# Second stage of a decoder layer in the order of use, with its first weights loaded in the stage before

## What is computed

```python
z = rmsnorm(x) @ w_in                        # q, kc, vc, ks, vs, kw, vw, gates, ...
def compress(t, pos, w1, w2):                # t is kc or vc: 2 groups of 64 columns
    blocks = t[:, win] + pos                 # 127 blocks of 32 tokens, one every 16
    return gelu(blocks.reshape(..., 32 * 64) @ w1) @ w2
kcmp, vcmp = compress(kc, ...), compress(vc, ...)
o_cmp = softmax(q @ kcmp - slope * dist) @ vcmp         # these scores also choose 8 blocks of 64 keys
o_sel = attention of q over the chosen blocks of ks, vs
o_win = attention of q over the last 512 keys of kw, vw
y_nsa = g0 * o_cmp + g1 * o_sel + g2 * o_win            # g = sigmoid(gates + gate_b)
```

## Time and profile before

| | us |
|---|---|
| median of 3 runs | 4426.35 |
| the profiled execution's own time | 4413.77 |
| its span | 4412.0 |
| first stage | 0 to 1562.0 |
| second stage | 1562.0 to 1645.4 |
| third stage until PE's first matmul | 1645.4 to 1663.3 |

### The profile page before, as it was taken

How to read it: one execution, slowest core, us unless ns; L and a number is a source line. 1 busy time by engine, 2 the same in 40 slices (tenths; PEclk the granted TensorE clock), 3 DMA queues, 4 the chain that set the end, 5 groups by cost and what they waited for, 6 DMA issues and landing times. The chain is left out here.

```text
span 4412.0 us, 69857 instructions
## 1 busy us (share of the span) xinstructions
PE 3913.7 (89%) x26848; PEld 3202.0 (73%) x26849; DVE 2436.8 (55%) x4140; ACT 1986.3 (45%) x3138; POOL 550.6 (12%) x842
## 2 busy tenths in 40 slices
PE   7899999999988848988888876999589999999698
PEld 5687877777766626777776765899578888888487
DVE  2454555555465426777766644444567555567465
ACT  2433333443332315666665643222166555566465
POOL 0111121111122002111111111000110000001110
PEclk9999999999999958999999966999789999999799
DMA  4443443433423250000000004433288666689542
GB/s 134 130 114 100 135 116 93 129 104 86 120 75 87 54 119 22 13 13 17 13 20 18 20 10 138 134 129 120 86 336 302 235 235 235 234 306 380 203 147 90
DMA packets 512951, 557.22 MB, mean 126 GB/s; under 512 B 106284, under 2 KB 374572, under 8 KB 511628
## 3 DMA queue, kind: packets, MB, share of 16 engines
q1 hardware_dynamic: 471476, 457.94, 32.6%
q0 software_dynamic: 16416, 59.78, 3.6%
q10 hardware_dynamic: 24784, 35.71, 2.5%
HBM read 439.78 MB, written 113.57 MB: 125 GB/s over the span
## 5 line engine op out<-in xcount | busy, mean ns | idle before, releaser
L523 PE MATMUL fr_fb<-fr_hT_h,fr_w_h 128*128 128x512 f32 (+1 forms) x1312 | 530.3, 404 | 7.7 <-DVE fr_hT_r L978 6.0
L523 PE MATMUL fr_fb<-fr_hT_r,fr_w_h 128*128 128x512 f32 (+1 forms) x1312 | 529.0, 403 | 0.0
L523 PE MATMUL fr_fb<-fr_hT_h,fr_w_r 128*128 128x512 f32 (+1 forms) x1312 | 528.2, 403 | 0.0
L958 DVE TENSOR_TENSOR fr_w_r<-fr_w_raw,fr_w_h 128x1024 fp32r<-128x1024 f32 (+1 forms) x164 | 197.7, 1206 | 487.6 <-ACT fr_w_h L774 486.5
L1911 DVE TENSOR_TENSOR aq_p_lo<-aq_t_bank,aq_p_hi 128x512 fp32r<-128x512 f32 x412 | 282.8, 689 | 225.9 <-ACT aq_p_hi L1804 220.0
L1804 ACT CAST aq_p_hi<-aq_t_bank 128x512 fp32r<-128x512 f32 x412 | 238.0, 581 | 293.7 <-PE aq_t_bank L1709 290.7
L798 ACT COPY fr_zs<-fr_fb 128x512 f32<-128x512 f32 (+1 forms) x148 | 87.1, 589 | 503.0 <-PE fr_fb L523 502.6
L523 PEld LDWEIGHTS fr_fb<-fr_hT_h,fr_w_h 128*128 128x128 f32 (+1 forms) x1312 | 246.8, 188 | 71.6 <-issue 10.4
L523 PEld LDWEIGHTS fr_fb<-fr_hT_h,fr_w_r 128*128 128x128 f32 (+1 forms) x1312 | 246.8, 188 | 62.8 <-issue 11.0
L134 PE MATMUL ex_gu<-wx_gate_w,ex_xT 128*128 128x512 f32 x1176 | 289.1, 402 | 3.0 <-DVE ex_xT L2667 3.0
L523 PEld LDWEIGHTS fr_fb<-fr_hT_r,fr_w_h 128*128 128x128 f32 (+1 forms) x1312 | 247.2, 188 | 61.3 <-issue 9.6
(11 more groups left out here) (474 smaller groups left out, 8787.5 us busy)
## 6 DMA issues: line engine op xcount, KB each, us to landing
wx_raw<-in_w_exp_gate_up SPq DMA_DIRECT2D x64, 2048.0 KB, 10.4
fr_w_raw<-in_w_in SPq DMA_DIRECT2D x160, 512.0 KB, 3.9
wx_raw<-in_w_exp_down SPq DMA_DIRECT2D x32, 2048.0 KB, 11.1
s_z<-fr_zs SPq DMA_DIRECT2D x160, 256.0 KB
s_rows<-ex_y ACTq DMA_DIRECT2D x50, 512.0 KB, 4.4
mx_mg<-s_z SPq DMA_DIRECT2D x32, 512.0 KB, 7.3
fr_zc<-s_z SPq DMA_DIRECT2D x15, 903.0 KB, 6.7
fr_x_t<-in_x SPq DMA_DIRECT2D x16, 512.0 KB, 5.5
```

Of the source, the lines that this page charges most:

```text
L523: ins = pe.matmul(bank[0:cols_, :], (w_h, w_h, w_r)[p][:, k, c, 0:cols_].bitcast(F32R), (hT_h, hT_r, hT_h)[p][:, c, :].bitcast(F32R), star ...
L958: dve.tensor_tensor(w_r[:, m % 2, :, 0:cols_].bitcast(F32R), w_raw[:, m % 2, :, 0:cols_], w_h[:, m % 2, :, 0:cols_], ALU.subtract).then_in ...
```

## The change

1. **A shared buffer.** `fr_x_t` becomes `sh_shared`, which lives through the first three stages. In its first 2080 columns `w1` and `pos` are placed, and in the third stage `t_sel`, `qf`, `t_cmp`, `keep_t` and `force_t` lie in it (`t_sel` over `w1` and `pos`, so it is still built in the third stage).
2. **Early weights.** SP issues the eight DMAs of `w1` and `pos` in the first stage, at the start of block 13, no longer ACT in the second.
3. **Order of use in the second stage.** `kv` of K is SP's first load and `kv` of V is ACT's first. PE multiplies with `pos` first, then `kv` of K, `kv` of V, V groups 0 to 3, the products with `w2`, V groups 4 to 7, the gates. ACT follows: gelu, 8 copies of V, then the four parts of K.
4. **Queries and tables.** The q loads of t = 15 and 14, the first three `qf`, both q splits and all tables but `t_sel` move into the second stage. `tab_ok` and the three waits for it go.

```diff
+                if c == NCH - 3:
+                    sync.wait_ge(filled, last_turn[NQ - 1] + 1)
+                    for a, n in enumerate(("k", "v")):
+                        for d in range(2):
+                            own = slice(d * HD, (d + 1) * HD)
+                            sync.dma_start(early["w1"][own, a, :, :], A[f"cmp_{n}_w1"][0]...).then_inc(early["in_w1"], 16)
+                            sync.dma_start(early["pos"][own, a, :], A[f"cmp_pos_{n}"][0]...).then_inc(early["in_w1"], 16)
...
             @block.sync
             def _(sync):
...
+                load_kv(sync, 0)
                 for br in range(2):
-                    sync.dma_start(v_raw[:, br, :], ...).then_inc(in_v, 16)
+                    sync.dma_start(v_raw[:, br, :], ...).then_inc(in_v[br], 16)
+                load_raw(sync, 0)
+                load_qf(sync, 0)
                 load_k(0)
                 load_k(1)
                 sync.dma_start(g_raw[:, :], Z["gate"]).then_inc(in_g, 16)
                 sync.dma_start(gate_b[:, :], ...).then_inc(in_g, 16)
+                load_raw(sync, 1)
                 load_k(2)
                 load_k(3)
+                for o in range(1, QF):
+                    load_qf(sync, o)
...
             @block.scalar
             def _(act):
...
+                load_kv(act, 1)
                 act.dma_start(w2_v[:, :], A["cmp_v_w2"][0]).then_inc(in_w, 16)
...
-                pe.wait_ge(tab_ok, 1)
...
-                act.wait_ge(tab_ok, 1)
...
-                dve.wait_ge(tab_ok, 1)
```

More of the change, by code:

```diff
@@ L1650, in _, with turn_v @@
                     masked(pair[:, :], [[-1, HD]], -d * HD, 1, 1.0, ALU.not_equal)
-                pool.sem_inc(tab_ok, 1)
+                split_q(pool, 0)
+                split_q(pool, 1)
+            @block.tensor
+            def _(pe):
+                def turn_v(n):
+                    pe.wait_ge(in_v[n // 4], 16)
+                    if n >= 4:
+                        pe.wait_ge(v_ok, n - 3)
+                    for t in range(4):
+                        ins = pe.transpose(tp[:, n % 4, t * P:(t + 1) * P],
+                                           v_raw[:, n // 4, (n % 4 * 4 + t) * P:(n % 4 * 4 + t + 1) * P], ident[:, :])
+                    ins.then_inc(turned, 1)
+                pe.wait_ge(in_w1, 16 * 8)
+                for a in range(2):
+                    for l in range(HALF):
+                        ins = pe.matmul(out[0:HD, POS + a:POS + a + 1], w1[:, a, l, :], pos[:, a, l:l + 1],
+                                        start=(l == 0), stop=(l == HALF - 1))
+                    ins.then_inc(pos_made, 1)
+                for a in range(2):
+                    both = acc[0:HD, a, 0:G * P].rearrange("p (g j) -> p g j", g=G)[:, :, 0:N_CMP]
+                    pe.wait_ge(in_kv[a], 32)
+                    for l in range(HALF):
+                        ins = pe.matmul(both, w1[:, a, l, :], kv[:, a, :, l:l + CMP_STRIDE * (N_CMP - 1) + 1:CMP_STRIDE],
+                                        start=(l == 0), stop=(l == HALF - 1))
+                    ins.then_inc(hid_made, 1)
+                pe.wait_ge(id_ok, 2)
+                for n in range(4):
+                    turn_v(n)
+                pe.wait_ge(hid_ok, 2 * G)
+                pe.wait_ge(in_w, 16 * 3)
+                for g in range(G):
+                    pe.matmul(out[:, 0:N_CMP], w2_k[:, g, :], hid[:, 0, g, :], start=(g == 0), stop=(g == G - 1))
+                for g in range(G):
+                    ins = pe.matmul(out[0:N_CMP, (2 + g) * P:(2 + g) * P + HD], hid[:, 1, g, :], w2_v[:, :],
+                                    start=True, stop=True)
+                ins.then_inc(out_made, 1)
+                for n in range(4, 8):
+                    turn_v(n)
+                pe.wait_ge(in_g, 32)
+                for t in range(NT):
+                    ins = pe.transpose(gp[:, t * N_GATE:(t + 1) * N_GATE], g_raw[:, t * P:(t + 1) * P],
+                                       ident[0:N_GATE, 0:N_GATE])
+                ins.then_inc(g_made, 1)
@@ new lines, in _, with high @@
+            @block.scalar
+            def _(act):
+                def high(i):
+                    br, g = i // G, i % G
+                    act.wait_ge(in_k[i % 2], 32 * (i // 2 + 1))
+                    act.copy(k_hi[:, br, g, :].bitcast(F32R), k_raw[:, i % 2, :]).then_inc(k_high, 1)
+                load_kv(act, 1)
+                act.dma_start(w2_v[:, :], A["cmp_v_w2"][0]).then_inc(in_w, 16)
+                act.wait_ge(w2_clear, 1)
+                for g in range(G):
+                    act.dma_start(w2_k[:, g, g * HD:(g + 1) * HD], A["cmp_k_w2"][0]).then_inc(in_w, 16)
+                act.wait_ge(pos_made, 2)
+                for a in range(2):
+                    act.copy(pos_p[:, a:a + 1], out[0:HD, POS + a:POS + a + 1]).then_inc(pos_ok, 1)
+                for a in range(2):
+                    act.wait_ge(hid_made, a + 1)
+                    act.wait_ge(pos_ok, a + 1)
+                    for g in range(G):
+                        act.activation(hid[:, a, g, :], acc[0:HD, a, g * P:g * P + N_CMP], ACT.Gelu_apprx_tanh,
+                                       bias=pos_p[:, a:a + 1]).then_inc(hid_ok, 1)
+                for n in range(8):
+                    act.wait_ge(turned, n + 1)
+                    act.copy(v2[:, n // 4, n % 4 * 4:n % 4 * 4 + 4, :, 0:HD].bitcast(F32R),
+                             tp[:, n % 4, :].rearrange("p (t g d) -> p t g d", t=4, g=G)).then_inc(v_high, 1)
+                high(0)
+                high(1)
+                act.wait_ge(g_ok, 1)
+                act.activation(gates[:, :, :], gates[:, :, :], ACT.Sigmoid).then_inc(g_done, 1)
+                high(2)
+                high(3)
+                act.wait_ge(g_done, 1)
@@ L3021, in build_program @@
         Z["passed"], Z["whole"] = passed, whole
-        stage_front(nc, A, Z)
-        stage_nsa(nc, A, Z)
+        with ExitStack() as both:
+            sh = Stage(nc, both, "sh")
+            shared = sh.sb("shared", [P, QCH, D])
+            early = dict(w1=shared[:, 0:2, :].rearrange("p a (l e) -> p a l e", e=HD),
+                         pos=shared[:, 2, 0:2 * L_HALF].rearrange("p (a l) -> p a l", a=2),
+                         in_w1=sh.lasting_sem("in_w1", whole))
+            stage_front(nc, A, Z, shared, early)
+            stage_nsa(nc, A, Z, shared, early)
         stage_moe(nc, A, Z)
```

357 lines of the change are left out of this document (149 added, 208 removed).

## The result

The changed kernel takes 4394.3 us (median of 4 runs, 4391.0 to 4401.6), the kernel before 4425.8 (4 runs, 4422.8 to 4428.9): a ratio of 0.9929 with a 95% interval of 0.9916 to 0.9942, or 31.5 us less (26 to 37). I forecast 4404.0 within 4392 to 4418, and gave faster by over 0.2% a chance of 0.87. The time fell in the range; the gain was 31.5 us where I had 22.4.

What follows compares the result with a forecast made beforehand. The prediction saw the second stage waiting for loads, then PE idle behind POOL's q split and tables. First attention matmul at 1640.9 instead of 1663.3 gains 22.4 us, less 0 in the first stage: 4426.35 - 22.4 = 4404.0, range 4392 to 4418.

Steps and rivals of the forecast that it cites:

- What bounds the kernel: Second stage waits for loads until about 1609; then PE idles 19.33 us behind POOL's q split and tables.
- The tables: Tables and q splits run on idle POOL under second-stage loads; PE no longer waits for them entering the third stage.
- The sum: First attention matmul at 1640.9 instead of 1663.32, a gain of 22.4 us, less 0 in the first stage.
- T: Start of the second stage, its first `kv` DMA; 1562.0 in the forecast's time line.
- The kv loads: Second stage's front: queues share 208 GB/s evenly, so K's and V's pairs land together at 1584.
- rival 1: Second stage: K's `kv` pair lands first, at 1574; gain 32.4 us, time 4394; chance 0.17.
- V: Second stage, behind the gelu: ACT's last V copy at 1619.5, within 1618.1 to 1621.8.
- K: Second stage's end: third and fourth K loads wait for `k_raw`'s buffers; last low part at 1640.0 instead of 1644.6.
- The change of stage: From DVE's last copy in the second stage to the third stage's first matmul: 0.9 us, giving 1640.9.
- `pos`: Second stage: PE's 4.6 us of products with `pos` run while `kv` is awaited, so hidden.
- The first stage: Block 13: the eight weight DMAs hold SP until about 1351, 4 us before the inverses' trip; 0 lost.
- rival 3: Block 13: small pieces starve the recurrence; slower by 0.2% needs 5.5 ns per piece, 60 us held gives 4450; chance 0.03.

Runs made afterwards that it cites:

- e1: Changed kernel with q's loads, both splits and the tables back in the third stage; 4409.1 us, ratio 0.9970 to before.
- e11: Kernel of e4 with K's `kv` pair first on both queues (lower half SP, upper ACT) and V's pair behind; 4381.4 us, ratio 0.9913.
- e4: Changed kernel with the first two K parts split between the two gelus; 4379.5 us, ratio 0.9908 to before.
- e2: Changed kernel with the eight `w1` and `pos` DMAs back on ACT's queue in the second stage, ahead of V's pair; 4426.5 us, ratio 1.0006.
- e5: Changed kernel with a second set of the eight weight DMAs behind the first in block 13; 4398.9 us, ratio 0.9944 to before.

## Why the prediction was right, and what was mis-sized

**What bounds the kernel: right.** Both stretches that I named were on the path. Undoing one costs 17.2 us, undoing the other 30.7.

**The tables: right.** I gave the moved tables and q the whole 17.9 us of idle time behind the stage; e1 gives 17.2. The cover that I named for q and the splits was there with room.

**The sum, step by step.** From T to attention I forecast 78.9 us and it took 72.65. The 6.3 us come from the first two terms; the others were met:
- *The kv loads*, 3.9 us. I took 1584 for both pairs, or +22, by an even share. The rate was right (220 where I had 208), the share was not: SP's pair ended 5.4 us ahead of ACT's. The first product started at +18.1, between the forecast and rival 1's +12, since V's pair is not needed until the second product. Rival 1's mechanism was at work in part. I had treated it as a case of its own and the even share as the likely one, with no row on either. That the median of 4394.3 is rival 1's 4394 is chance: its condition, K's pair at +12, did not come true, and even with K first on both queues (e11) it is there only at +15.2. One reading was wrong: the trace of before does have two queues with 64-partition loads in flight. From 1603.83, when SP issues K loads, to 1608.1, when V's upper half lands on ACT's queue, 204 GB/s move. So the 208 of the earlier trace rows is not `kv` alone, and it agrees with the rule on the halves; how two queues share is still not in it.
- *V*, 2.3 us. From the first product to ACT's last V copy I had 35.5 us and it took 33.2. The transposes took 1.97 us for 16, where the earlier trace rows has 3.65 at 1.2 GHz; PE had come from 27.6 us of work, and from 1621.2 to 1626.2 its granted clock is 1.00 (2.4 GHz). I knew the lower end of that range (1618.1) and took a value 1.4 us above it. The other 0.9 us lie below that end: mostly the products with `w2`, which held PE for 1.0 us (1623.16 to 1624.18) where I had 2.2.
- *K*: 20.5 us forecast from the last V copy to the last low part, 20.4 measured. The reload behind `k_raw`'s two buffers was the end of the stage, as the prediction had it, and e4 shows that it was so by order alone: it gives 12.3 us back by splitting two parts while ACT and DVE stood idle. The prediction said that nothing hides these loads, and did not ask what else could.
- *The change of stage*: 0.9 and 0.9.
- *`pos`* was hidden, as forecast, but it takes 6.96 us at 1.2 GHz and not 4.6; e2 shows it when it is not hidden.

**The first stage: nearly right.** I took nothing lost. SP was held 10.3 us instead of 7.6 to 8.2, mostly by one of `pos` (3.13 us). The margin of the trip was all but used up (SP is free at 1366.73 and issues the trip at 1367.41); but the trip itself took 2.8 us more, its pieces being in the queue with the weights' last ones, and that step I had not looked at. It cost DVE 1.2 us and PE 1.35. e5 shows that the price of one more microsecond there is about one, as rival 3 says; its 5.5 ns a piece was far from the 1.3 measured (10.3 us for 8192).

**The rest.** 28.7 us in the second stage less 1.2 in the first are 27.5; the medians differ by 31.5, with an interval of 26 to 37. The 4 us between are within that interval and within the scatter of the rest: in thirteen profiled executions the way from the first attention matmul to the end takes 2747.2 to 2758.6 us, and in the changed kernel's it is 2.9 us longer than in before's, not shorter. Where the 4 us come from stays open.

## What to carry to other kernels

When a stage is shortened at its front, list what was hidden under that front and ask who is idle there: the loads that became the new end here could be split in idle time, 12 us earlier, by moving four lines. Changes on one path don't add: undone one at a time, the early weights and the early tables cost 30.7 and 17.2 us, and the whole change brought 28.7. What each is worth has to be told with what stands beside it. And where a tensor has to be written in two DMAs of 64 partitions, look whether its partitions may be permuted: every second one instead of a half took the loads from 220 to 411 GB/s.
